# Causal attention in groups of 512 queries, with V stationary, instead of blocks of 128 queries

## The reference

```
def _causal_attention(q, k, v):            # q, k: (1, 4, 2064, 192), v: (1, 4, 2064, 128)
    scale = 1.0 / math.sqrt(dq)
    def one_block(args):                   # one block of 128 queries
        qb, start = args
        s = jnp.einsum("bhqd,bhkd->bhqk", qb, k).astype(jnp.float32) * scale
        mask = key_pos[None, :] <= q_pos[:, None]
        p = jax.nn.softmax(jnp.where(mask, s, -jnp.inf), axis=-1)
        return jnp.einsum("bhqk,bhkd->bhqd", p.astype(v.dtype), v)
```

## Time and profile before

| | us |
|---|---|
| median of 3 runs (lowest, highest) | 3686.16 (3685.36, 3688.68) |
| the profiled execution, own time | 3679.25 |
| its span, first to last instruction | 3677.8 |
| attention stage in it, from the identity made at 1278.8 to the out stage's first instruction at 1829.3 | 550 |

### The profile page before, as it was taken

The page is one execution under the profiler, slowest core; times in us unless marked ns, Lnnn a source line. Parts: engine busy times, 40 slices in busy tenths (PEclk is TensorE's granted clock), DMA queues, the critical chain, the costliest instruction groups (busy, mean ns, idle before and its releaser), DMA issues. The chain is left out here.

```text
span 3677.8 us, 55042 instructions
## 1 busy us (share of the span) xinstructions
PE 3235.0 (88%) x20547; PEld 2695.5 (73%) x20547; DVE 1603.7 (44%) x2494; ACT 1219.9 (33%) x2323; POOL 580.3 (16%) x971
## 2 busy tenths in 40 slices
PE   7995749993999789999759959999999999999998
PEld 6884548993777657766547748887888788878887
DVE  2114633432444366566477624432454245424542
ACT  3213522222344344445333324422332133213321
POOL 1112420003656300000045410000000000000000
PEclk9997879996899889999879979999999999999999
DMA  5443454222343240120046542244433433343322
GB/s 164 144 131 98 120 187 155 78 73 62 80 88 82 66 125 28 57 65 29 20 156 210 171 144 80 80 137 132 112 99 126 133 109 100 125 133 108 102 80 103
DMA packets 408414, 394.58 MB, mean 107 GB/s; under 512 B 42458, under 2 KB 333734, under 8 KB 405302
## 3 DMA queue, kind: packets, MB, share of 16 engines
q1 hardware_dynamic: 369286, 286.21, 26.8%
q0 software_dynamic: 26240, 91.67, 7.9%
q10 hardware_dynamic: 12720, 14.42, 1.2%
HBM read 284.92 MB, written 107.30 MB: 107 GB/s over the span
## 5 line engine op out<-in xcount | busy, mean ns | idle before, releaser
L2224 DVE TENSOR_TENSOR ff_w_lo<-ff_w_raw,ff_w_hi 128x2048 fp32r<-128x2048 f32 (+1 forms) x176 | 309.2, 1759 | 573.0 <-ACT ff_w_hi L2189 573.0
L2189 ACT ACTIVATE ff_w_hi<-ff_w_raw 128x2048 fp32r<-128x2048 f32 (+1 forms) x176 | 261.8, 1488 | 495.2 <-PE ff_pD L2304 346.3
L2282 PE MATMUL ff_pG<-ff_u_hi,ff_w_hi 128*128 128x512 f32 x704 | 278.4, 395 | 34.5 <-DVE ff_w_lo L2224 34.5
L2304 PE MATMUL ff_pD<-ff_w_hi,ff_g_hi 128*128 128x512 f32 x704 | 274.6, 390 | 4.5 <-DVE ff_yb L2254 3.5
L2282 PE MATMUL ff_pG<-ff_u_lo,ff_w_hi 128*128 128x512 f32 x704 | 277.5, 394 | 0.0
L2282 PE MATMUL ff_pG<-ff_u_hi,ff_w_lo 128*128 128x512 f32 x704 | 277.3, 394 | 0.0
L2282 PE MATMUL ff_pU<-ff_u_hi,ff_w_hi 128*128 128x512 f32 x704 | 276.4, 393 | 0.0
L2282 PE MATMUL ff_pU<-ff_u_hi,ff_w_lo 128*128 128x512 f32 x704 | 274.3, 390 | 0.0
L2282 PE MATMUL ff_pU<-ff_u_lo,ff_w_hi 128*128 128x512 f32 x704 | 274.0, 389 | 0.0
L2304 PE MATMUL ff_pD<-ff_w_lo,ff_g_hi 128*128 128x512 f32 x704 | 274.0, 389 | 0.0
L2304 PE MATMUL ff_pD<-ff_w_hi,ff_g_lo 128*128 128x512 f32 x704 | 273.9, 389 | 0.0
(11 more groups left out here) (346 smaller groups left out, 6893.8 us busy)
## 6 DMA issues: line engine op xcount, KB each, us to landing
ff_w_raw<-in_w_gate SPq DMA_DIRECT2D x88, 512.0 KB, 4.0
ff_w_raw<-in_w_up SPq DMA_DIRECT2D x88, 512.0 KB, 5.2
ff_w_raw<-in_w_down SPq DMA_DIRECT2D x176, 256.0 KB, 2.9
scr_tok<-pj_tok POOLq DMA_DIRECT2D x17, 548.0 KB, 3.1
scr_uT<-pj_u_hi POOLq DMA_DIRECT2D x17, 512.0 KB, 4.6
scr_uT<-pj_u_lo POOLq DMA_DIRECT2D x17, 512.0 KB, 6.6
scr_yT<-cv_y SPq DMA_DIRECT2D x8, 1088.0 KB, 4.0
scr_dtok<-cv_ob SPq DMA_DIRECT2D x8, 1088.0 KB, 5.7
```

Of the source, the lines that this page charges most:

```text
L2189: act.activation(w_hi[s][:, 0:w], w_raw[s][:, 0:w], ACT.Copy).then_inc(w_half[s], 1)
L2224: dve.tensor_tensor(w_lo[s][:, 0:w], w_raw[s][:, 0:w], f(w_hi[s][:, 0:w]), ALU.subtract).then_inc(w_ready[s], 1)
L2282: m = pe.matmul(bank[s][:, :], a[s][:, o:o + P], x[:, k, :], start=(k == 0 and n_pass == 0), stop=(k == KD - 1 and n_pass == 2))
L2304: m = pe.matmul(pD[t][:, :], x[:, ft, t * P:t * P + P], a[s][:, i * 512:i * 512 + 512], start=(ft == 0 and n_pass == 0), stop=(ft == FT - ...
```

## The change

Only the attention stage and its V layout change; the other stages are the same code.

- **Grid.** The 16 meta tokens are a key tile of their own, and the 2048 positions are 16 tiles of 128 for queries and keys. The 16 meta queries of all heads are done once by small matmuls at the start of the stage.
- **Groups.** Work goes in 16 groups n = (head, g), g = 0 to 3, of 512 queries (four rows of 128). A group has STEPS = 4(g + 1) + 1 steps: step 0 is the 16 meta keys, every other step 128 keys. Steps past the diagonal leave out the queries that don't see them, so the last four steps are 512, 384, 256 and 128 wide.
- **Values.** `values(n, m)` holds V stationary (v_hi, v_lo, v_hi) and streams the transposed exponentials, 512 queries at a time, into one bank `pO`, which is feature-major (128 features x 512 queries). At a group's end ACT copies it to `oT` (L1683), TensorE turns it back with four transposes (L1863), and DVE divides (L1786).
- **Scores.** Row i has (128(i + 1) + 16) keys, cut into pieces as even as whole tiles allow: 44 per head, 17,664 keys in all (before: 45 chunks, 19,584 keys). The pieces of group n + 1 are spread over the first STEPS - 2 steps of group n (`issued`).
- **Transposes** run two steps ahead, with three `pT` banks and three pairs `pt_hi`, `pt_lo`. The first step of group n + 1 is turned in the last step of group n and needs all four exponentials of n + 1, which are now taken in place in one buffer per row.
- **Loads.** K, rotary key and V come in quarters of a head, and their splits are spread over steps. Nothing loops: the stage is written out in full.

```diff
-                act.dma_start(S["v"][:, :, bass.ds(t, 1), :].rearrange("h p j d -> p (h j) d"), kv[s][:, :, NOPE:]).then_inc(v_stored[s], 16)
+                act.dma_start(S["v"][:, bass.ds(t * P, P), :].rearrange("h p d -> p h d"), kv[s][:, :, NOPE:]).then_inc(v_stored[s], 16)
...
+        def issued(n, m):
+            if n + 1 == NG:
+                return []
+            count, room = len(PIECES[ORDER[n + 1][1]]), STEPS[n] - 2
+            return [k for k in range(count) if k * room // count == m]
...
+        def turns(n, m):
+            out = []
+            if m == 0:
+                out = [(n, 1), (n, 2)]
+            elif m + 2 < STEPS[n]:
+                out = ([(n - 1, None)] if m == 1 and n else []) + [(n, m + 2)]
+            if m == STEPS[n] - 1 and n + 1 < NG:
+                out.append((n + 1, 0))
+            return out
...
-            def values(p, b, g):
...
-                pe.wait_ge(lo_done, CT * p + m + 1)
-                for j in range(4 * g, min(4 * g + 4, i + 1)):
-                    n = j - 4 * g
-                    pe.matmul(pO[b % 2][:, 0:2 * VD], pt_hi[m % 2][:, n, :], v[h][:, j, :, :].rearrange("p a d -> p (a d)"),
-                              start=(j == 0), stop=False)
-                    t = pe.matmul(pO[b % 2][:, 0:VD], pt_lo[m % 2][:, n, :], v[h][:, j, 0, :],
-                                  start=False, stop=(j == i))
...
+            def values(n, m):
+                h, g = ORDER[n]
+                x, at = SB[n] + m, P * first_tile(m - QB * g)
+                pe.wait_ge(t_used, x + 1)
...
+                for y, (a, p) in enumerate(((v_hi, pt_hi), (v_lo, pt_hi), (v_hi, pt_lo))):
+                    t = pe.matmul(pO[n % 2][:, at:GW], a, p[x % NPX][part, at:GW], start=(m == 0 and y == 0),
+                                  stop=(m == STEPS[n] - 1 and y == 2), skip_group_check=True)
                 t.then_inc(pv_done, 1)
...
+            pe.wait_ge(m_loaded, 80)
+            for h in range(HEADS):
+                cols = slice(h * N_META, h * N_META + N_META)
+                pe.matmul(pO[0][0:N_META, cols], qkm[:, 0, h, :], qkm[:, 1, h, :], start=True, stop=False)
+                t = pe.matmul(pO[0][0:N_META, cols], qkm_rope[:, 0, h, :], qkm_rope[:, 1, h, :], start=False, stop=True)
...
+            turn(0, 0)
+            for n in range(NG):
+                for m in range(STEPS[n]):
+                    for tn, tm in turns(n, m):
+                        turn(tn, tm)
+                    for k in issued(n, m):
+                        scores(n + 1, k)
+                    values(n, m)
+            turn(NG - 1, None)
```

More of the change, by code:

```diff
@@ new lines, in stage_attention, with cut @@
+        NPS, NPT, NPX = 3, 3, 3
+        WIDEST = [max(N_META + P * (QB * g + i + 1) for _, g in ORDER[x::2] for i in range(QB)) for x in range(2)]
+        def cut(i):
+            nb = i + 1
+            n = -(-(P * nb + N_META) // 512)
+            base, extra = divmod(nb, n)
+            at, out = 0, []
+            for k in range(n):
+                end = at + P * (base + (k >= n - extra)) + (N_META if k == 0 else 0)
+                out.append((i % QB, k, at, end, k == n - 1))
+                at = end
+            return out
@@ new lines, in turns @@
+        def turns(n, m):
[6 more added lines that the diff above has]
+                out.append((n + 1, 0))
+            return out
+        TURN = {x: i for i, x in enumerate([(0, 0)] + [x for n in range(NG) for m in range(STEPS[n]) for x in turns(n, m)]
+                                           + [(NG - 1, None)])}
@@ new lines, in stage_attention @@
+        q_lo = [r.sb(f"q_lo{i}", [P, GW], F32R) for i in range(2)]
+        qr_hi = [r.sb(f"qr_hi{i}", [P, GW], F32R) for i in range(2)]
+        qr_lo = [r.sb(f"qr_lo{i}", [P, GW], F32R) for i in range(2)]
+        rows = [[r.sb(f"row{i}_{j}", [P, WIDEST[i] - P * (QB - 1 - j)]) for j in range(QB)] for i in range(2)]
+        pt_hi = [r.sb(f"pt_hi{i}", [P, GW], F32R) for i in range(NPX)]
+        pt_lo = [r.sb(f"pt_lo{i}", [P, GW], F32R) for i in range(NPX)]
+        most = [r.sb(f"most{i}", [P, QB, 8]) for i in range(2)]
@@ new lines, in _ @@
+            split_q(1)
+            hi(0, 0)
+            for n in range(NG):
+                for m in range(STEPS[n]):
+                    if m == 0 and n:
+                        outputs(n - 1)
+                    for tn, tm in turns(n, m):
+                        if tm is not None:
+                            hi(tn, tm)
+                    if m:
+                        for i in finished(n, m - 1):
+                            exp(n + 1, i)
+                    if m == 1 and n + 2 < NG:
+                        split_q(n + 2)
+                    for h, x in SPLIT_AT.get((n, m), []):
+                        split(h, x)
@@ new lines, in _ @@
+            for n in range(NG):
+                for m in range(STEPS[n]):
+                    for tn, tm in turns(n, m):
+                        if tm is None:
+                            norm(tn)
+                        else:
+                            lo(tn, tm)
+                    for k in issued(n, m):
+                        scores(n + 1, k)
+                    if m == 0:
+                        inverse(n)
+                    if m == 1 and n + 2 < NG:
+                        split_q(n + 2)
+                    for h, x in SPLIT_AT.get((n, m), []):
+                        split(h, x)
@@ L1715, in _ @@
+            norm(NG - 1)
         @block.tensor
@@ new lines, in _ @@
+            for h in range(HEADS):
+                t = pe.transpose(pO[1][0:N_META, h * N_META:h * N_META + N_META], sm[3][:, h, :], ident[0:N_META, 0:N_META])
+            t.then_inc(meta_pe, 1)
+            pe.wait_ge(meta_act, 2)
+            for h in range(HEADS):
+                t = pe.matmul(pO[0][0:N_META, h * VD:h * VD + VD], sm_turned[:, h, :], vm_raw[:, h, :], start=True, stop=True)
+            t.then_inc(meta_pe, 1)
+            turn(0, 0)
+            for n in range(NG):
+                for m in range(STEPS[n]):
+                    for tn, tm in turns(n, m):
+                        turn(tn, tm)
+                    for k in issued(n, m):
+                        scores(n + 1, k)
+                    values(n, m)
```

566 lines of the change are left out of this document (305 added, 261 removed).

## The result

| | us |
|---|---|
| after, median of 4 runs (lowest, highest) | 3627.98 (3620.25, 3629.30) |
| before, median of 4 runs on the same chip | 3687.42 (3685.36, 3692.20) |
| ratio, with 95% interval | 0.9833 (0.9815 to 0.9850) |
| the profiled execution of after, own time | 3628.79 |
| attention stage in it, identity to the out stage's identity | 492.3 (before 550.9) |

The account below looks back on a forecast made before the run. TensorE was taken to pace the attention stage: start 1306 + work 408 + waits 37 + clock 26 + open 7 = 1784, + 9.9 + 3 = 1797, 32 us less; 3647 plus 6.9 gives 3654 us, range 3613 to 3695.

Parts of the forecast that it names:

- it goes better: Rival: exponential chain partly hidden, clock hardly falling (25 + 10 for 37 + 26), nothing open; 3619 us, chance 0.13.
- TensorE's work: Attention stage's scores, values, transposes and 16-row matmuls summed by row prices: 408 us after, against 452.5 before.
- values in steps of 0.70 to 0.71: Sign to look for: each full step's three 512-column value matmuls take this many us; above 0.75 would be wrong.
- The 7 us carried over: Part of TensorE's old 519.8 us stretch that the sum of 513 left open, added unchanged to the forecast.
- Group changes: TensorE waits for the next group's four exponentials: 1.9, 2.3 and 2.9 us, four times each, 28 us.
- VectorE's 5 + 4 us: Waits from VectorE running late: 5 us at starts of g = 3 groups, 4 us for g = 0 and the first head.
- Clock: Loss from TensorE's lowered clock over the stretch: 26 us kept from before, with ends 10 and 56.
- the clock eats it: Rival: each of twelve group changes is followed by a clock fall, clock 56 instead of 26; 3684 us, chance 0.10.
- Start and end: Stage's ends: first scores at 1290, first transpose at 1306; the 9.9 us tail lengthened by 3.
- +3: At the stage's end, 3 us added to the 9.9 us tail because the store is four times as large.
- Handover pace: Rival: in steps without scores the 0.25 us margin breaks, 176 steps each wait 0.3 more; 3707 us, chance 0.10.
- Doesn't do what it says: Rival: the change might not deliver its claimed work; only a hidden saving was left, judged none; no chance given.

Follow-up runs that it names:

- a_again: The changed kernel unaltered, run again as comparison point for later variants; ratio 0.9838 to the kernel before, stage 497.6 us.
- b_no_tile17: The kernel before without the 17th block of queries of each head (last 16 positions not computed); ratio 0.9863 to the kernel before.
- b_unrolled: The kernel before with the attention stage's loop of two passes written out, nothing else changed; ratio 0.9992 to the kernel before.
- a_scores_late: The changed kernel with the next group's scores spread over STEPS - 1 steps instead of STEPS - 2; ratio 0.9850 to the kernel before.
- a_filled: The changed kernel with ten extra identity transposes ahead of each TensorE wait for a new group's exponentials; ratio 0.9801 to the kernel before.
- a_one_ahead: The changed kernel with transposes one step ahead of the values instead of two; ratio 0.9868 to the kernel before.
- a_scores_early: The changed kernel with the next group's scores issued over STEPS - 4 steps (at least 2) instead of STEPS - 2; ratio 0.9772 to the kernel before.
- a_old_values: The changed kernel with values in the old form, transposed exponentials stationary, 8 matmuls for 4 tiles instead of 3; ratio 0.9867 to the kernel before.
- a_warm: a_best plus 64 extra identity transposes at the start of the stage, during the wait for first loads; ratio 0.9726 to the kernel before.
- a_best: The changed kernel with scores over STEPS - 4 steps (STEPS - 2 where STEPS is 5) and a reordered start; ratio 0.9768 to the kernel before.

## Why the prediction was right, and where it was off

The stage was to take 518.6 us from its identity (1278.4 to 1797) and took 492.3: 26.3 too many in the sum. The other stages took 8 us more than before in this execution, so its own time is 18 off (3647 for 3629). The median was put 6.9 above the profiled execution, the offset of before; it lies 0.8 below it: 8 more, which makes 26. The 4.8 us ahead of the stage are how executions vary: in a_again the stage begins at 1275.3 and in after at 1283.2. For the 3.3 behind it that isn't shown: the nine kernels made from after have 1848.4 to 1851.8 us there, the three made from before 1846.1 to 1848.5. The measured 3628 lies nearer to the rival *it goes better* (3619) than to the forecast (3654).

- **TensorE's work: right, by errors that cancel in part.** 408 predicted, 410.6 measured, and a step as a whole has the price reckoned (1.14 for 1.13). Its parts don't: the sign that the prediction names, values in steps of 0.70 to 0.71 and wrong above 0.75, was not met, since by their starts they take 0.79 and the transposes 0.35. The values save 25.6 for 30 (34 less the meta steps), and the work of before was 459.4, not 452.5. Where the prediction calls the 16 us of scores "almost all of it the 17th tile that was padding", it hides what b_no_tile17 shows: the tile is worth 51.5 in all, 27 of them scores by the same prices (4 x 6.75), and the new grid takes 11 of the 27 back.
- **The 7 us carried over: wrong.** This is the step "7 us of 519.8 stay open, and I carry them over". By the split above they were work of the old form (459.4 against 452.5), as in b_unrolled and b_no_tile17 (460.6, and 407.9 where the same prices give 402); what work, no run shows. In the new form only 2.6 of them are there. 4 us of the miss.
- **Group changes: the mechanism right, the size a little too long (4 us of the miss).** Twelve waits, in three lengths, as named: 1.9, 2.3 and 2.9 predicted, 1.55, 1.97 and 2.53 measured, 24.2 us for 28. Most of it lies in two terms of the chain: from VectorE's start to the masked part 0.35 (1351.49 to 1351.84), not 0.50, and from the exponential's end to the transposes 0.23 (1354.50 - 1352.68 - 1.59), not 0.32. a_scores_late confirms the chain by its dose, 0.52 us longer for the step taken away.
- **VectorE's 5 + 4 us: wrong.** Not one wait for `pt_lo` came. In after the start of g = 3 ran at half clock, which would hide a late VectorE; but a_filled goes through it at full clock, and has 0.2 us of them. The ledger of six steps left out that VectorE enters them without arrears and with two steps of lead; that this is the reason is argued, not tested. 9 us of the miss, the largest term. a_one_ahead shows that even half that lead costs only some 10 us.
- **Clock: the size right, by luck in part.** 26 predicted; 58.1 us at half clock at 0.45 are 26.1, and in the repetition 31.6. The argument was that "not each was followed by a fall". Eight of twelve were, against seven falls in before, which had 56.0 us of half clock for the 58.1. That is nearer to the mechanism of the rival *the clock eats it* than the forecast has it; the rival priced every fall at the 4.7 us of the earlier trace rows, ten us at half clock, and half of the eight last 3.4 us. Why the sum stayed the same is not shown.
- **Start and end: 4 and 5 us too long.** First transposes 23.5 us after the identity, not 27.6. The rows of the start, for the earlier trace rows:

```profile
1292.07 0.21 PE L1903 MATMUL at_pO<-at_qkm 128*16 128x16 f32 x2 [13.62 <-DMA at_vm_raw<-scr_v]
1292.12 0.71 DVE L1740 TENSOR_TENSOR at_kr<-at_kr_raw,at_kr 64x528 fp32r<-64x528 f32 x1
...
1293.36 0.49 PE L1851 MATMUL at_pS<-at_k_hi,at_q_hi 128*128 128x144 f32 x1
...
1304.37 0.40 ACT L1667 ACTIVATE at_row<-at_row,at_stat 128x144 f32<-128x144 f32 x1
...
1306.74 0.53 PEld L1870 LDWEIGHTS at_pT<-at_ident,at_row 128*16 128x16 f32 x4 [0.83 <-ACT at_row L1667]
```

The scores began 10.15 us after the identity (11.6 predicted) and took 8.9 (9 predicted); from their end to the first exponential are 2.1 us (3 predicted), and the four exponentials with their sums took 2.4 (3.1 predicted). The small loads let TensorE go at 1292.07, and VectorE's last split for these scores ended at 1292.83, so without the small loads and the meta matmuls the scores could, by these rows, have begun 0.5 us earlier. That bounds what the 64-byte pieces cost. The Trainium skill's 512 B for line rate, which the prediction cites, stands on its page DMA: Bandwidth & Descriptors under Specifications. No run here isolates it, and the start came early, not late. The end:

```profile
1768.73 0.63 PE L1863 MATMUL at_pT<-at_ident,at_oT 128*128 128x128 f32 x4 [0.78 <-ACT at_oT L1683]
1769.39 0.69 DVE L1787 TENSOR_TENSOR at_o_sb<-at_pT,at_stat 128x512 f32<-128x512 f32 x1 [2.05 <-PE at_pT L1863]
1770.38 0.75 POOL L1626 DMA_DIRECT2D scr_o_mla<-at_o_sb  x1 [18.17 <-DVE at_o_sb L1787]
1775.52 0.20 POOL L117 MEMSET ot_ident<- 128x128 f32 x1 [4.38 <-POOLq L2463]
```

The store is four times as large, and the out stage starts 4.38 us after it is issued; before, 7.97. "+3" had the wrong sign. The loop is excluded (7.94 in b_unrolled); what the 8 us are stays open.

- **Rivals.** *Handover pace*, 3707: a_one_ahead provokes its mechanism, and even there it is 12 us (6.0 idle and 5.5 of work), not 53. *It goes better*, 3619: of its terms the changed kernel has the waits (24.6 for 25) and not the clock (26 for 10); a_scores_early goes below both, with 15.6 idle and 12 us of clock. *The clock eats it*, 3684: the clock cost 26, not 56. *Doesn't do what it says*: excluded by b_no_tile17 and a_old_values, each with its share of the work.

## What to carry to other kernels

When TensorE paces a stage, price each of its waits twice: for its length, and for the clock behind it, which here cost as much again (24.6 us idle, 26 us of clock) and went at every group change when the waits were filled, a little over half, with matmuls that nobody needs. Issue the work whose result a group change depends on early enough that several full steps lie behind it; one number in the order (STEPS - 4 for STEPS - 2) was worth some 23 us by the ratios, four tenths of the whole rewrite. And count what padding costs before praising a new form: leaving out the padded tile alone gave 50 us, where the whole rewrite gave 59. The new grid cost some 33 us of work, and the new form of the values earned 26 of them back.

## What the hardware showed that was not expected

How often TensorE's clock fell in a wait or soon behind it, by the wait's length, in the twelve traces of this study (attention stage from where the clock first rises; waits over 1 us, none of them under 1.2):

| wait of TensorE, us | waits | followed by half clock |
|---|---|---|
| 1.22 to 1.44 | 24 | 3 |
| 1.55 to 1.61 | 28 | 10 |
| 1.75 to 1.87 | 12 | 7 |
| 1.97 to 2.32 | 28 | 23 |
| 2.42 to 6.15 | 23 | 23 |

The wait of 1.33 us in a_warm, which begins behind a fall, is left out. So there is no sharp length in these traces: behind the same wait of 1.55 us the clock fell once in four times in a_best and in a_again, and not at all in after and a_warm. Behind a wait near 1.5 us the clock fell about one time in three, behind one over 2.4 every time. The Trainium skill, TensorE: Matmul & The Clock Gate, section HAM oscillation, warns of idle gaps longer than any of the twelve waits of after; by that rule none would have cost clock. The rows of after and of a_filled say that they did, and the measurement decides.

The same kernel can also carry 3.5 or 19.2 us of half clock behind the same start (after and a_again), 7 us of difference between executions from that alone, with TensorE busy for nearly all of it. And of the 0.235 us from one 512-column matmul to the next: it is 0.24 in after too (1759.72 to 1759.96). The Trainium skill, TensorE: Matmul & The Clock Gate, section Back-to-back issue gap, gives its 216 ns for 512 columns as the gap of an isolated matmul, and about 131 ns for a sustained stream. The rows are above both, and the 7 us that the prediction worked out from the 216 ns did not come.
